# Pooling layer in channel order: one 512-wide product for both halves of the activation, and window sums as shifted additions

## The chip, the cores and the metric

The kernel runs on one core of a Trainium2 chip. The metric is the device time of one execution in microseconds; the time before is the median of three runs.

## The reference, cut to what matters

A token sequence (256 tokens, 2048 channels) passes a retention layer, a pooling layer and a second, longer block. The change is in the pooling layer:

```python
h = rms_norm(x, g_norm)                       # a factor for each token, one for each channel
u, z = jnp.split(h @ w_in, [POOL_WIDTH], axis=-1)
# four groups of 1024 channels, windows w = 2, 4, 8, 16
for gi, w in enumerate(POOL_WINDOWS):
    lo = jnp.maximum(t + 1 - w, 0)
    cnt = jnp.minimum(t + 1, w)
    pooled_gi = (cs[t + 1] - cs[lo]) / cnt    # mean of the last w tokens
mix = jnp.einsum('bsgc,gcd->bsgd', pooled - u, w_grp) + b_grp
out = (mix.reshape(B, S, POOL_WIDTH) * scale * silu(z)) @ w_out
```

## The kernel before

All weights come as one stream of 900 chunks of 256 x 512 numbers (512 KB). A chunk goes through five hands, each engine working its own program in order, and rings of four slots (`raw`, `whi`, `wlo`) couple them: SyncE starts the transfer into `raw`, ScalarE casts `raw` to `whi` (line 626), VectorE subtracts to get the rest `wlo` (line 1078), TensorE multiplies. ScalarE and VectorE prepare chunk j + 4 in iteration j, the cast waiting until TensorE has finished chunk j (`multiplied`), since that frees the slot. A product of full precision takes three matmuls: high x high, high x low, low x high. The activation too is held in two halves (`aH`, `aL`).

In `chunk_a` (lines 1930 to 1932) the activation is the stationary operand and the 512 columns of the chunk stream past it: 12 matmuls of 512 columns, and the result has a token on each partition. In `chunk_b` (lines 1955 to 1958, used in the second block) the weights are stationary and the 256 tokens stream: 24 matmuls of 256 columns, and the result has a channel on each partition. Both make the same products.

The pooling layer takes four groups of 40 chunks (`group`, `first` for group 0), then the product with the output weights (128 chunks of `chunk_a` on `oH`, `oL`). In a group, chunks 0 to 15 give u (two halves of 512 channels, `b` = 0 and 1), chunks 16 to 31 give z, chunks 32 to 39 multiply the pooled input by the group's weights. Before the change the pooling itself is a matrix product: after chunk 19, 32 matmuls (lines 2056 to 2059) take u, split into `pUH` and `pUL`, times a 256 x 256 band matrix `pMH`, and turn it into channel order. ScalarE makes `pUH` (line 660, scaled with each token's `rstd`), `pMH` (742) and then `mH` (747); VectorE makes `pUL` (1301) and `mL` (1308). At the end of each half of the group's product, in iterations 35 and 39, VectorE waits for the chunk, adds the bias in two instructions that read the result (`mz`, line 1320, semaphore `mz_add`), and gates with silu(z) (`pZ`, line 1328). In the next group's first 16 iterations it turns the result into `mz_turned` (line 1092) and splits it (`oL`, line 1114).

The order on every engine is what the code spells out; nothing is planned at run time.

Of the kernel before, what the change touches and what calls it, by code (L numbers as in the profile page):

```python
# [101 lines left out]
C_END = C_WIN + GROUPS * NT  # L102
# [7 lines left out]
def build(nc, dram):  # L110
    with ExitStack() as outer:
# [19 lines left out]
        aH = sb(outer, "aH", [P, 16, SEQ], F32R)  # L131
        aL = sb(outer, "aL", [P, 16, SEQ], F32R)
# [17 lines left out]
        with ExitStack() as s:  # L150
# [20 lines left out]
            with ExitStack() as r:  # L171
                with ExitStack() as b:
                    mz = sb(b, "mz", [P, NT, NB])
                    pB = sb(b, "pB", [P, GDIM])
                pUH = sb(r, "pUH", [P, NT, GDIM], F32R)
                pUL = sb(r, "pUL", [P, NT, GDIM], F32R)
# [5 lines left out]
                pM = sb(r, "pM", [P, 3 * P])  # L182
                pMH = sb(r, "pMH", [P, 3 * P], F32R)
# [7 lines left out]
        with ExitStack() as s:  # L191
# [89 lines left out]

        cum_rows = nc.dram_tensor("cum_rows", [NT, DN_HEADS, P], F32).ap()
# [27 lines left out]
        pu_sb, pu_lo, pz_sb, mix_ps, mix_hi, mix_lo, pm_in, pb_in, mz_add, mz_sb, pb_used = (  # L310
            sem(n) for n in "pu_sb pu_lo pz_sb mix_ps mix_hi mix_lo pm_in pb_in mz_add mz_sb pb_used".split())
# [189 lines left out]
        def _(pool):  # L501
# [79 lines left out]
            pool.wait_ge(const_set, 3)  # L581
# [37 lines left out]
        def _(act):  # L619
# [107 lines left out]
            def group(i, first):  # L727
                q = i * (P_PER // RING) + P_AT // RING
                for j in range(P_PER):
                    split_hi(q, j + RING)  # L730
                    if first and j == 1:
                        t_split_hi(T_N2 + 3, aH, 12, lambda c: C_PN + 12 + c)
                    if not first and j in (8, 16):
                        group_tail(i - 1, j // 8 - 1)
                    if j in (7, 15):
                        done(act, q, j)
                        b = j // 8
                        act.wait_ge(row_rstd, M_N2 + 1)
                        by_token(pUH[:, :, b * NB:(b + 1) * NB], 2 * b, ACT.Copy, M_N2, pu_sb)
                    if j == 16:  # L740
                        act.wait_ge(pm_in, i * 16 + 16)
                        nc.scalar.copy(pMH[:], pM[:]).then_inc(pu_sb, 1)
                    if j == 19:
                        act.wait_ge(t_lo, (T_P + 2 * i) * QT)
                        for b in range(4):
                            act.wait_ge(mix_ps, i * 4 + (b + 1))
                            nc.scalar.copy(mH[:, 2 * b:2 * b + 2].rearrange("p a n -> p (a n)"),
                                           PS[:, 4 + b]).then_inc(mix_hi, 1)
                    if j in (23, 31):
                        done(act, q, j)  # L750
                        b = j // 8 - 2
                        by_token(pZ[:, :, b * NB:(b + 1) * NB], 2 * b, ACT.Silu, M_N2, pz_sb)
# [173 lines left out]
            def first_tap(i):  # L926
# [6 lines left out]
                act.wait_ge(const_set, 4)  # L933
# [139 lines left out]
        def _(dve):  # L1073
# [212 lines left out]

            def group(i, first):
                q = i * (P_PER // RING) + P_AT // RING
                for j in range(P_PER):
                    split_lo(q, j + RING)  # L1290
                    if first and j == 1:
                        t_split_lo(T_N2 + 3, aH, aL, 12, lambda c: C_PN + 12 + c)
                    if not first:
                        after_group(i - 1, j, 2)
                    if j in (7, 15):

                        b = j // 8
                        dve.wait_ge(pu_sb, i * 3 + (b + 1))
                        for t in range(NT):
                            cut = pUH[:, t, b * NB:(b + 1) * NB].bitcast(F32)  # L1300
                            ins = nc.vector.scalar_tensor_tensor(out=pUL[:, t, b * NB:(b + 1) * NB], in0=PS[:, 2 * b + t],
                                                                 scalar=rstd[:, M_N2, t:t + 1], in1=cut, op0=ALU.mult,
                                                                 op1=ALU.subtract)
                        ins.then_inc(pu_lo, 1)
                    if j == 19:
                        for b in range(4):
                            dve.wait_ge(mix_hi, i * 4 + (b + 1))
                            nc.vector.tensor_tensor(mL[:, 2 * b:2 * b + 2].rearrange("p a n -> p (a n)"), PS[:, 4 + b],
                                                    mH[:, 2 * b:2 * b + 2].rearrange("p a n -> p (a n)").bitcast(F32),
# [604 lines left out]
        def _(pe):  # L1914
# [46 lines left out]

            def transpose_tiles(src, bank=6):
# [74 lines left out]
            def group(i, first):  # L2037
                q = i * (P_PER // RING) + P_AT // RING
                for j in range(4 * K16):
                    b = j // K16  # L2040
                    if j == 16 or j == 24:
                        pe.wait_ge(pu_lo, i * 2 + (b - 1))
                    if first and j == 6:
                        pe.wait_ge(t_lo, (T_N2 + 4) * QT)
                    chunk_a(q, j, (j % K16) * KPC, aH, aL, 2 * (b % 2), j % K16 == K16 - 1)
                    if first and j == 1:
                        pe.wait_ge(h_out, 2 + 4)
                        pe.wait_ge(t_lo, (T_N2 + 3) * QT)
                        transpose_tiles(quarter(H, 3))
                    if j == 19:  # L2050

                        pe.wait_ge(pu_lo, i * 2 + 2)
                        pe.wait_ge(pu_sb, i * 3 + 3)
                        for c in range(8):
                            out, ch = half(4, c), slice(c * P, (c + 1) * P)
# [432 lines left out]
```

## Time and profile before

| | |
|---|---|
| median of 3 runs | 2625.68 us (2625.46 to 2626.24) |
| span of the profiled execution | 2624.1 us |
| TensorE busy | 2608.1 us, 99% of the span |
| VectorE busy | 1960.0 us, 75% |
| ScalarE busy | 1321.0 us, 50% |
| DMA | 499.69 MB, 190 GB/s on average |

The profiled execution's own time is not given apart from the runs; the three runs stand 1.4 to 2.1 us above its span, which is what lies around first and last instruction. "Busy" of TensorE counts overlapped matmuls once; the duration of one matmul in the profile is its latency, so its pace has to be read from the starts of successive ones.

### The profile page before, as it was taken

What the parts mean: (1) busy time and instruction counts of PE and PEld (TensorE: products, weight loads), DVE (VectorE), ACT (ScalarE), POOL (GpSimd) and SP (SyncE); (2) the same over time, 40 slices, a digit from 0 to 9 for tenths busy, and PEclk for the clock granted to TensorE, in tenths of its full rate; (3) what the DMA queues carried; (4) which work ended last, traced back from release to release, by engine and by line L of the source; (5) the groups of instructions that cost most, each with busy time, mean ns of one, the idle gap of its engine ahead of it and who ended that gap; (6) DMA issues with size and microseconds to landing.
All of it is one profiled execution on the core that took longest, in us unless ns stands there. A gap on an engine that the chain in (4) does not pass through costs nothing.

```text
span 2624.1 us, 36684 instructions
## 1 busy us (share of the span) xinstructions
PE 2608.1 (99%) x13284; PEld 2218.9 (85%) x13284; DVE 1960.0 (75%) x2764; ACT 1321.0 (50%) x1683; POOL 168.0 (6%) x329
## 2 busy tenths in 40 slices
PE   9999999999999999999999999999999999999998
PEld 7888888888888888888889999998888888788887
DVE  5888877776755766757457786977798999989565
ACT  5444444444444544444456454454666666564453
POOL 0000000000000000000000341413000000000000
PEclk9999999999999999999999999999999999999999
DMA  8555555555655555556655555655555655655754
GB/s 309 179 187 177 179 185 185 184 191 190 198 193 192 195 196 192 196 185 217 196 189 176 173 165 159 194 159 175 176 197 191 197 192 187 200 188 194 247 175 159
DMA packets 151674, 499.69 MB, mean 190 GB/s; under 512 B 28736, under 2 KB 29472, under 8 KB 151008
## 3 DMA queue, kind: packets, MB, share of 16 engines
q1 hardware_dynamic: 148736, 486.18, 56.0%
q0 software_dynamic: 2784, 11.40, 1.4%
q8 instruction: 104, 1.70, 0.3%
q14 instruction: 50, 0.41, 0.0%
HBM read 493.30 MB, written 4.21 MB: 190 GB/s over the span
## 4 chain that ended last, share of the span: by engine, by line
PE 97%; DVE 2%; ACT 1%; issue 0%; DMA 0%; POOL 0%; SPq 0%; DVEq 0%; ACTq 0%
PE PS L1930 27%; PE PS L1932 27%; PE PS L1931 27%; PE PS L1955 4%; PE PS L1957 4%; PE PS L1958 4%; PE PS L2096 2%; DVE yl L1624 1%; DVE wlo L1078 0%; PE PS L2103 0%; PE PS L1966 0%; PE PS L2112 0%; DVE yl L1615 0%; PE PS L2010 0%; PE PS L2020 0%
## 5 line engine op out<-in xcount | busy, mean ns | idle before, releaser
L1078 DVE TENSOR_TENSOR wlo<-raw,whi 128x1024 fp32r<-128x1024 f32 x899 | 1096.9, 1225 | 595.8 <-ACT whi L626 591.1
L626 ACT CAST whi<-raw 128x1024 fp32r<-128x1024 f32 x899 | 939.6, 1049 | 1180.7 <-PE PS L1932 1009.4
L1930 PE MATMUL PS<-whi,aH 128*128 128x512 f32 x2160 | 844.1, 391 | 3.2 <-DVE wlo L1137 1.9
L1931 PE MATMUL PS<-wlo,aH 128*128 128x512 f32 x2160 | 840.6, 389 | 0.0
L1932 PE MATMUL PS<-whi,aL 128*128 128x512 f32 x2160 | 840.6, 389 | 0.0
L1930 PEld LDWEIGHTS PS<-whi,aH 128*128 128x128 f32 x2160 | 405.6, 188 | 88.1 <-issue 2.3
L1932 PEld LDWEIGHTS PS<-whi,aL 128*128 128x128 f32 x2160 | 405.5, 188 | 84.6
L1931 PEld LDWEIGHTS PS<-wlo,aH 128*128 128x128 f32 x2160 | 405.6, 188 | 82.9
L1955 PE MATMUL PS<-aH,whi 128*128 128x256 f32 x768 | 220.8, 288 | 1.5 <-DVE aL L1114 1.5
L1957 PE MATMUL PS<-aL,whi 128*128 128x256 f32 x768 | 217.1, 283 | 0.0
L1958 PE MATMUL PS<-aH,wlo 128*128 128x256 f32 x768 | 217.1, 283 | 0.0
L1932 PE MATMUL PS<-whi,oL 128*128 128x512 f32 x512 | 199.2, 389 | 0.0
L1930 PE MATMUL PS<-whi,oH 128*128 128x512 f32 x512 | 199.2, 389 | 0.0
L1931 PE MATMUL PS<-wlo,oH 128*128 128x512 f32 x512 | 199.2, 389 | 0.0
L1955 PEld LDWEIGHTS PS<-aH,whi 128*128 128x128 f32 x768 | 147.0, 191 | 2.5 <-issue 1.7
L1957 PEld LDWEIGHTS PS<-aL,whi 128*128 128x128 f32 x768 | 147.2, 192 | 0.1
L1958 PEld LDWEIGHTS PS<-aH,wlo 128*128 128x128 f32 x768 | 147.0, 191 | 0.0
L1624 DVE SCALAR_TENSOR_TENSOR yl<-up,wl,yl 128x256 f32<-128x256 f32 x272 | 113.3, 478 | 0.2
L1931 PEld LDWEIGHTS PS<-wlo,oH 128*128 128x128 f32 x512 | 96.1, 188 | 20.1
L1932 PEld LDWEIGHTS PS<-whi,oL 128*128 128x128 f32 x512 | 96.1, 188 | 20.1
L1930 PEld LDWEIGHTS PS<-whi,oH 128*128 128x128 f32 x512 | 96.1, 188 | 19.6
L1930 PE MATMUL PS<-whi,oaH 128*128 128x512 f32 x256 | 99.9, 390 | 0.0
(357 smaller groups left out, 2570.6 us busy)
## 6 DMA issues: line engine op xcount, KB each, us to landing
raw<-in_stream SPq DMA_DIRECT2D x900, 512.0 KB, 3.3
xT<-in_xT SPq DMA_DIRECT2D x4, 512.0 KB, 7.6
H<-in_x SPq DMA_DIRECT2D x4, 512.0 KB, 10.0
pB<-in_pool_b POOLq DMA_DIRECT2D x4, 512.0 KB, 4.5
iT<-diag_in SPq DMA_DIRECT2D x16, 128.0 KB, 3.7
bg<-in_b_gate POOLq DMA_DIRECT2D x8, 256.0 KB, 3.8
out<-eb SPq DMA_DIRECT2D x8, 256.0 KB, 2.2
dmask<-in_dmask SPq DMA_DIRECT2D x4, 384.0 KB, 5.8
```

The source lines that it names most:

```text
L626: nc.scalar.copy(whi[:, s], raw[:, s]).then_inc(hi_done, 1 + blank)
L1078: nc.vector.tensor_tensor(wlo[:, s], raw[:, s], whi[:, s].bitcast(F32), ALU.subtract).then_inc(lo_done, 1 + blank)
L1624: nc.vector.scalar_tensor_tensor(out=to, in0=up[:, c, k:k + SEQ], scalar=w, in1=yl[:, c], op0=ALU.mult, op1=ALU.add).then_inc(long_tap[c], 1)
L1930: mm(out, hi[:, kt + k, tok], whi[:, s, k], start=kt + k == 0, stop=False)
L1931: mm(out, hi[:, kt + k, tok], wlo[:, s, k], start=False, stop=False)
L1932: ins = mm(out, lo[:, kt + k, tok], whi[:, s, k], start=False, stop=last and k == KPC - 1)
L1955: mm(half(bank, c), whi[:, s, k, w], aH[:, kt + k], start=kt + k == 0 and c % 2 == 0, stop=False, skip_group_check=True)
L1957: mm(half(bank, c), whi[:, s, k, w], aL[:, kt + k], start=False, stop=False, skip_group_check=True)
L1958: ins = mm(half(bank, c), wlo[:, s, k, w], aH[:, kt + k], start=False, stop=end, skip_group_check=True)
L2096: ins = mm(PS[rows, bank + n, h * P + at:h * P + at + width], lhsT(t, h), rhs(t, h), start=h == 0, stop=True, skip_group_check=True)
```

## The change

- `aH` and `aL` become two interleaved parts of one tile `aHL`, so that both halves of the activation are 512 contiguous columns.
- u is computed by a new function `chunk_w`: weights stationary, a matmul of 512 columns for `whi` against both halves, one of 256 columns for `wlo` against the high half. The two halves of a bank are added on VectorE (`pU`), and then multiplied by a row of the tokens' `rstd` (`rrow`, fetched through DRAM).
- The band product is gone. VectorE forms window sums by 1, 2, 3 or 4 shifted additions between padded tiles (`window_sum`), subtracts size times u, and treats the first tokens apart.
- The eight PSUM banks are dealt out anew: u in banks 4 to 7 (b = 0) and 0 to 3 (b = 1), z in banks 4 to 7. TensorE gets new waits for that, `mz_add` among them: in front of chunk 8 of groups 1 to 3, and in front of the output product.

```diff
+ADD_AT = (9, 17)
+SUM_AT = ((11, 13, 15, 18, 19, 20), (21, 23, 24, 25, 26, 27))
+SPLIT_AT = (22, 29)
...
                     if j in (7, 15):
                         done(act, q, j)
                         b = j // 8
-                        act.wait_ge(row_rstd, M_N2 + 1)
-                        by_token(pUH[:, :, b * NB:(b + 1) * NB], 2 * b, ACT.Copy, M_N2, pu_sb)
-                    if j == 16:
-                        act.wait_ge(pm_in, i * 16 + 16)
-                        nc.scalar.copy(pMH[:], pM[:]).then_inc(pu_sb, 1)
-                    if j == 19:
+                        act.wait_ge(const_set, 3)
+                        if not first:
+                            act.wait_ge(mix_lo, i * 2 + (b - 1))
+                        nc.scalar.copy(pU[:, b, :, PAD:], wide(b)[:, :, SEQ:]).then_inc(pu_lo, 1)
+                    if j + 1 in SPLIT_AT:
+                        b = SPLIT_AT.index(j + 1)
                         act.wait_ge(t_lo, (T_P + 2 * i) * QT)
-                        for b in range(4):
-                            act.wait_ge(mix_ps, i * 4 + (b + 1))
-                            nc.scalar.copy(mH[:, 2 * b:2 * b + 2].rearrange("p a n -> p (a n)"),
-                                           PS[:, 4 + b]).then_inc(mix_hi, 1)
+                        act.wait_ge(pool_step, steps_before(i, b + 1))
+                        nc.scalar.copy(mH[:, b * QT:(b + 1) * QT], pU[:, b, :, PAD:]).then_inc(mix_hi, 1)
...
+            def window_sum(i, b, n):
+
+                at, early = steps_before(i, b) + n, POOL_WINDOWS[i] - 1
+                u = pU[:, b, :, PAD:]
+                if n == 0:
+                    if i == 0 and b == 0:
+                        dve.wait_ge(rrow_in, 32)
+                    dve.wait_ge(pu_sb, i * 2 + (b + 1))
+                    nc.vector.tensor_tensor(u, u, rrow[:, None, :].to_broadcast([P, QT, SEQ]), ALU.mult).then_inc(pool_step, 1)
+                    return
+                dve.wait_ge(pool_step, at)
+                shift = 1 << (n - 1)
+                v = pU[:, b] if n == 1 else pS[:, n % 2]
+                if n <= i + 1:
...
+                    nc.vector.tensor_tensor(pS[:, (n + 1) % 2, :, PAD:], v[:, :, PAD:], v[:, :, PAD - shift:PAD - shift + SEQ],
+                                            ALU.add).then_inc(pool_step, 1)
+                else:
...
+                    nc.vector.tensor_tensor(own_size, u[:, :, 0:early], sizes, ALU.mult).then_inc(pool_step, 1)
+                    nc.vector.scalar_tensor_tensor(out=u[:, :, early:], in0=u[:, :, early:], scalar=float(-POOL_WINDOWS[i]),
+                                                   in1=v[:, :, PAD + early:], op0=ALU.mult, op1=ALU.add).then_inc(pool_step, 1)
+                    dve.wait_ge(pool_step, at + 1)
+                    nc.vector.tensor_tensor(u[:, :, 0:early], own_size, v[:, :, PAD:PAD + early], ALU.add).then_inc(pool_step, 1)
...
+            def chunk_w(q, j, kt, b, last):
...
+                for k in range(KPC):
+                    for c in range(QT):
+                        w, out = slice(c * P, (c + 1) * P), wide(b)[:, c]
+                        mm(out, whi[:, s, k, w], aHL[:, kt + k].rearrange("p a n -> p (a n)"), start=kt + k == 0, stop=False,
+                           skip_group_check=True)
+                        ins = mm(out[:, 0:SEQ], wlo[:, s, k, w], aH[:, kt + k], start=False, stop=last and k == KPC - 1,
+                                 skip_group_check=True)
+                ins.then_inc(multiplied, 1)
...
             for i in range(1, P_N):
                 group(i, False)
+            pe.wait_ge(mz_add, P_N * 2)
             for b in range(4):
                 q = (PO_AT + b * K32) // RING
                 pe.wait_ge(h_out, 4 + b + 1)
```

TensorE, before: the pooling product behind chunk 19 of a group (`aH`, `aL` belong to the chunk, `pUH`, `pUL` and `pMH` to the product).

```order
L1930 MATMUL PS<-whi,aH 128x512
L1931 MATMUL PS<-wlo,aH 128x512
L1932 MATMUL PS<-whi,aL 128x512
L2056 MATMUL PS<-pMH,pUH 128x256 [waits pu_sb,pu_lo]
L2057 MATMUL PS<-pMH,pUL 128x256
L2058 MATMUL PS<-pMH,pUH 128x128
L2059 MATMUL PS<-pMH,pUL 128x128
L2056 MATMUL PS<-pMH,pUH 128x256
```

TensorE, now: the first rows of a chunk of u in `chunk_w`.

```order
L2018 MATMUL PS<-aHL,whi 128x512 [waits lo_done]
L2020 MATMUL PS<-aHL,wlo 128x256
L2018 MATMUL PS<-aHL,whi 128x512
L2020 MATMUL PS<-aHL,wlo 128x256
L2018 MATMUL PS<-aHL,whi 128x512
```

The 32 matmuls of the product have no successor on TensorE; a chunk of u has 16 matmuls (8 wide, 8 narrow) where it had 12 wide ones.

TensorE, before: the last matmuls of group 3 and the first of the output product.

```order
L1930 MATMUL PS<-whi,mH 128x512
L1931 MATMUL PS<-wlo,mH 128x512
L1932 MATMUL PS<-whi,mL 128x512
L1930 MATMUL PS<-whi,oH 128x512 [waits lo_done,h_out]
L1931 MATMUL PS<-wlo,oH 128x512
```

TensorE, now, at the same place.

```order
L1978 MATMUL PS<-whi,mH 128x512
L1979 MATMUL PS<-wlo,mH 128x512
L1980 MATMUL PS<-whi,mL 128x512
L1978 MATMUL PS<-whi,oH 128x512 [waits lo_done,h_out,mz_add]
L1979 MATMUL PS<-wlo,oH 128x512
```

The order is the same, but the first matmul of the output product now also waits for `mz_add`.

VectorE, before: group 3, iterations 16 to 39 (`wlo` is the split of a chunk).

```order
L1114 SCALAR_TENSOR_TENSOR oL<-mz_turned,cols,oH 128x256 [waits t_hi] x4
L1078 TENSOR_TENSOR wlo<-raw,whi 128x1024 [waits hi_done] x3
L1308 TENSOR_TENSOR mL<-PS,mH 128x512 [waits mix_hi] x4
L1078 TENSOR_TENSOR wlo<-raw,whi 128x1024 [waits hi_done] x16
L1320 SCALAR_TENSOR_TENSOR mz<-PS,cols,pB 128x512 [waits mz_sb,pb_in,multiplied]
```

VectorE, now: group 3, iterations 17 to 22.

```order
L1351 TENSOR_TENSOR pU<-PS,pU 128x4x256 [waits pu_lo]
L1103 TENSOR_TENSOR wlo<-raw,whi 128x1024 [waits hi_done]
L1328 TENSOR_TENSOR pS<-pS 128x4x256 [waits pool_step]
L1103 TENSOR_TENSOR wlo<-raw,whi 128x1024 [waits hi_done]
L1328 TENSOR_TENSOR pS<-pS 128x4x256 [waits pool_step]
L1103 TENSOR_TENSOR wlo<-raw,whi 128x1024 [waits hi_done]
L1333 TENSOR_TENSOR pS<-pU,cols 128x4x15 [waits pool_step]
L1334 SCALAR_TENSOR_TENSOR pU<-pU,pS 128x4x241
L1337 TENSOR_TENSOR pU<-pS 128x4x15 [waits pool_step]
L1103 TENSOR_TENSOR wlo<-raw,whi 128x1024 [waits hi_done]
L1320 TENSOR_TENSOR pU<-pU,rrow 128x4x256 [waits pu_sb]
L1103 TENSOR_TENSOR wlo<-raw,whi 128x1024 [waits hi_done]
```

Where VectorE did split after split, a full-size instruction now stands behind each split.

## Rows read from the trace of the kernel before

**Rows 1.** The page: span, busy time and granted clock in 40 slices.
```profile
span 2624.1 us, 36684 instructions
...
PE 2608.1 (99%) x13284; PEld 2218.9 (85%) x13284; DVE 1960.0 (75%) x2764; ACT 1321.0 (50%) x1683; POOL 168.0 (6%) x329
...
PEclk9999999999999999999999999999999999999999
```

**Rows 2.** Waits of PE in the whole span: us in total, times, longest.
```profile
PE PS L1930 <- DVE wlo L1137: 1.9, 1, 1.9
...
PE PS L1930 <- DVE wlo L1078: 1.4, 1, 1.4
```

**Rows 3.** Timeline of PE around group 0's pooling product: start, duration (us).
```profile
788.75 0.28 PE L2056 MATMUL PS<-pMH,pUH 128*128 128x256 f32 x1
...
789.15 0.33 PE L2056 MATMUL PS<-pMH,pUH 128*128 128x256 f32 x1
789.32 0.28 PE L2057 MATMUL PS<-pMH,pUL 128*128 128x256 f32 x1
...
792.40 0.45 PE L1930 MATMUL PS<-whi,aH 128*128 128x512 f32 x1
792.68 0.40 PE L1931 MATMUL PS<-wlo,aH 128*128 128x512 f32 x1
```

**Rows 4.** Tile pUH: min/median/max ns, first and last start (us).
```profile
L2056 PE MATMUL PS<-pMH,pUH x32: 277/332/333, 788.7 to 1129.5; 128*128 128x256 f32 x32
```

**Rows 5.** Timeline where the last group ends and the output product begins.
```profile
1184.45 0.39 PE L1930 MATMUL PS<-whi,oH 128*128 128x512 f32 x1
...
1184.71 1.05 ACT L626 CAST whi<-raw 128x1024 fp32r<-128x1024 f32 x1 [1.67 <-PE PS L1932]
...
1185.79 1.23 DVE L1078 TENSOR_TENSOR wlo<-raw,whi 128x1024 fp32r<-128x1024 f32 x1 [1.50 <-ACT whi L626]
...
1186.93 1.40 DVE L1320 SCALAR_TENSOR_TENSOR mz<-PS,cols,pB 128x512 f32<-128x512 f32 x2
...
1187.17 0.39 PE L1930 MATMUL PS<-whi,oH 128*128 128x512 f32 x1
```

**Rows 6.** Timeline of PE in chunk_b: a chunk, first row to next.
```profile
1374.03 0.28 PE L1955 MATMUL PS<-aH,whi 128*128 128x256 f32 x1
...
1376.91 1.03 PE L1966 MATMUL PS<-con,XS 128*128 128x128 f32 x8
```

**Rows 7.** Timeline: a stall of PE that a wlo ends.
```profile
2261.78 1.21 DVE L1078 TENSOR_TENSOR wlo<-raw,whi 128x1024 fp32r<-128x1024 f32 x1
...
2263.05 0.50 PE L1930 MATMUL PS<-whi,aH 128*128 128x512 f32 x1 [1.37 <-DVE wlo L1078]
...
2263.38 0.40 PE L1931 MATMUL PS<-wlo,aH 128*128 128x512 f32 x1
...
2263.62 0.39 PE L1932 MATMUL PS<-whi,aL 128*128 128x512 f32 x1
```

**Rows 8.** Groups between 720 and 1260 us: count, busy us, mean ns, idle before.
```profile
L1078 DVE TENSOR_TENSOR wlo<-raw,whi 128x1024 fp32r<-128x1024 f32 x193 | 235.9, 1225 | 184.4 <-ACT whi L626 183.7
L626 ACT CAST whi<-raw 128x1024 fp32r<-128x1024 f32 x193 | 202.0, 1049 | 276.5 <-PE PS L1932 275.5 <-DMA raw<-in_stream 0.9
...
L1092 DVE STREAM_TRANSPOSE mz_turned<-pZ 32x256 f32<-32x256 f32 x128 | 55.8, 436 | 2.5
...
L1114 DVE SCALAR_TENSOR_TENSOR oL<-mz_turned,cols,oH 128x256 fp32r<-128x256 f32 x32 | 13.3, 478 | 0.0
...
L1320 DVE SCALAR_TENSOR_TENSOR mz<-PS,cols,pB 128x512 f32<-128x512 f32 x16 | 11.2, 743 | 0.0
...
L1347 DVE TENSOR_TENSOR H<-PS,H 128x1024 f32<-128x1024 f32 x1 | 1.2, 1218 | 0.0
```

**Rows 9.** Windows at the start: us, then busy us (x instructions) by engine, PEclk, DMA.
```profile
3.00:4.00 1.00, 1.00 (x7) 1.00 (x7) 0.00 (x0) 0.00 (x0) 0.00 (x0) 1.00 0.97 181
...
5.00:6.00 1.00, 1.00 (x12) 1.00 (x11) 0.00 (x0) 0.09 (x1) 0.00 (x0) 1.00 1.00 360
```

More of the change, by code:

```diff
@@ L366, in half, with wide, steps_before @@
             return PS[:, bank + c // 2, (c % 2) * SEQ:(c % 2 + 1) * SEQ]
+        def wide(b):
+            return PS[:, 4 - 4 * b:8 - 4 * b]
+        def steps_before(i, b):
+            return sum(2 * (g + 5) for g in range(i)) + b * (i + 5)
         def heads(bank):
@@ L932, in first_tap @@
                 act.wait_ge(up_sb, i + 1)
-                act.wait_ge(const_set, 4)
+                act.wait_ge(const_set, 5 + P_N)
                 act.wait_ge(wl_set, i + 1)
@@ L1291, in group @@
                     if first and j == 1:
-                        t_split_lo(T_N2 + 3, aH, aL, 12, lambda c: C_PN + 12 + c)
+                        t_split_lo(T_N2 + 3, aH, aL, 12, lambda c: C_PN + 12 + c, 0)
                     if not first:
                         after_group(i - 1, j, 2)
[L1295 to L1309, printed above, removed]
+                    for b in range(2):
+                        if j == ADD_AT[b]:
+                            dve.wait_ge(pu_lo, i * 2 + (b + 1))
+                            u = pU[:, b, :, PAD:]
+                            nc.vector.tensor_tensor(u, wide(b)[:, :, 0:SEQ], u, ALU.add).then_inc(pu_sb, 1)
+                        if j in SUM_AT[b][:i + 3]:
+                            window_sum(i, b, SUM_AT[b].index(j))
+                        if j == SPLIT_AT[b]:
+                            dve.wait_ge(mix_hi, i * 2 + (b + 1))
+                            nc.vector.tensor_tensor(mL[:, b * QT:(b + 1) * QT], pU[:, b, :, PAD:],
+                                                    mH[:, b * QT:(b + 1) * QT].bitcast(F32),
                                                     ALU.subtract).then_inc(mix_lo, 1)
@@ L2040, in group @@
                     b = j // K16
-                    if j == 16 or j == 24:
-                        pe.wait_ge(pu_lo, i * 2 + (b - 1))
+                    if j == 0:
+                        if not first:
+                            pe.wait_ge(pz_sb, i * 2)
+                    if j == K16 and not first:
+                        pe.wait_ge(mz_add, i * 2)
+                    if b >= 2 and j % K16 == 0:
+                        pe.wait_ge(pu_sb, i * 2 + (b - 1))
                     if first and j == 6:
                         pe.wait_ge(t_lo, (T_N2 + 4) * QT)
-                    chunk_a(q, j, (j % K16) * KPC, aH, aL, 2 * (b % 2), j % K16 == K16 - 1)
+                    if b < 2:
+                        chunk_w(q, j, (j % K16) * KPC, b, j % K16 == K16 - 1)
+                    else:
+                        chunk_a(q, j, (j % K16) * KPC, aH, aL, 2 * b, j % K16 == K16 - 1)
                     if first and j == 1:
@@ L2048, in group @@
                         pe.wait_ge(t_lo, (T_N2 + 3) * QT)
[L2049 to L2055, printed above, removed]
-                            mm(out, pUH[:, 0, ch], pMH[:, 0:SEQ], start=c % 2 == 0, stop=False, skip_group_check=True)
-                            mm(out, pUL[:, 0, ch], pMH[:, 0:SEQ], start=False, stop=False, skip_group_check=True)
-                            mm(out[:, P:], pUH[:, 1, ch], pMH[:, SEQ:], start=False, stop=False, skip_group_check=True)
-                            ins = mm(out[:, P:], pUL[:, 1, ch], pMH[:, SEQ:], start=False, stop=True,
-                                     skip_group_check=True)
-                            if c % 2:
-                                ins.then_inc(mix_ps, 1)
-                pe.wait_ge(mix_lo, i * 4 + 4)
+                        transpose_tiles(quarter(H, 3), 0)
                 for w in range(2):
-                    pe.wait_ge(pz_sb, i * 2 + (w + 1))
                     for k in range(4):
+                        if not w and k % 2 == 0:
+                            pe.wait_ge(mix_lo, i * 2 + (k // 2 + 1))
                         chunk_a(q, 4 * K16 + 4 * w + k, k * KPC, mH, mL, 2 * w, k == 3)
```

63 lines of the change are left out of this document (40 added, 23 removed).

## Prediction

> **What bounds the kernel now.** First the page: TensorE is busy 2608.1 of 2624.1 us, at full clock in all 40 slices [rows 1]. Then TensorE's waits: the longest is 1.9 us, at the start, and the one behind it 1.4 us, near 2263 us; none lies in the pooling stage [rows 2]. So nobody but TensorE sets the end: a microsecond that it is spared or made to idle there is a microsecond of the result, and work on the other engines costs nothing until it makes TensorE wait. Its pace comes from starts, since durations overlap: a chunk of `chunk_a`, 12 matmuls of 512 columns, takes from 1184.45 to 1187.17, 2.72 us [rows 5]. In the stage VectorE is idle 184 us ahead of its splits and ScalarE 277 us ahead of its casts, nearly all of it until TensorE frees a slot [rows 8]. That is the cover for what the change adds on them.
>
> **The pooling product goes.** Its first matmul starts at 788.75, chunk 20 at 792.40: 3.65 us. The first matmul of chunk 20 is followed after 0.28 us where 0.23 is usual, 0.05 more [rows 3]. 32 of L2056 [rows 4], eight to a group, make four such products. 4 x 3.70 = 14.8 us saved, all on the path.
>
> **A chunk of u gets four more matmuls for the same columns.** 8 x 512 + 8 x 256 = 6144 = 12 x 512. What the split costs is read from `chunk_b`, which has the same 6144 columns in 24 matmuls: 1374.03 to 1376.91, 2.88 us [rows 6]. That is 0.16 us over `chunk_a` for 12 matmuls more, 13.3 ns each. Four more make 0.053 us, on 4 x 16 = 64 chunks 3.4 us. No row shows a wide and a narrow matmul in turn with weights on both. Bounds: nothing (columns alone count), and the longest spacing of a 256-column one, 0.17 us (789.15 to 789.32), which follows a 128-column one [rows 3]; against 0.12 in `chunk_b` that is 0.05 x 8 x 64 = 26 us. I take 3.4, since here every narrow matmul stands behind a wide one, longer than the 0.12 at which `chunk_b` gets its weights in.
> The Trainium skill, "TensorE: Matmul & The Clock Gate", section "Back-to-back issue gap", gives a start-to-start gap of N / 2.4 + 2.5 ns at full clock. By that an extra matmul costs 2.5 ns, the 64 chunks 0.6 us, and the sum below would end 2.8 us lower. The rows disagree with it here (13 ns a matmul), and I go by them.
>
> **The wait in front of the output product.** TensorE's program now has `wait_ge(mz_add, P_N * 2)` ahead of the first matmul on `oH`, that is, it waits for the last `mz` of group 3. VectorE makes that in iteration 39, behind the split of chunk 43, which waits for the cast, which waits until TensorE is through with chunk 39. The rows give the whole chain, as nothing in it changes: TensorE could go on at 1184.45; cast from 1184.71, split from 1185.79, the two `mz` from 1186.93 for 1.40, to 1188.33 [rows 5]. Before, TensorE multiplied through this (chunks 40 and 41), since banks 0 and 1 had been read in iteration 35. Now it idles 3.88 us. Leaving a stall costs more: in the one at 2263 the split ends at 2262.99, TensorE starts at 2263.05, and the next start comes after 0.33 instead of 0.23, the one after it 0.24 [rows 7]: 0.06 + 0.11. Together 4.05 us. Nothing gives it back, as TensorE has no slack behind it; what is queued behind the waiting matmul is the entire output product. ScalarE and VectorE only gain time by it.
>
> **The other new waits of TensorE** cost nothing. `mz_add` at chunk 8 of groups 1 to 3 asks for the same event, 3.9 us after the end of chunk 39, with 8 x 2.72 = 21.8 us to spare it. `pz_sb` at chunk 0: silu of iteration 31. `pu_sb` at chunks 16 and 24: the additions of iterations 9 and 17, six chunks earlier. `mix_lo` at chunks 32 and 34: splits in iterations 22 and 29; the later starts, undelayed, 1.34 + 1.23 us after chunk 29 ends [rows 5] and takes 1.22, so 3.8 of the 10.9 us (four chunks) to chunk 34's start.
>
> **VectorE.** It loses eight `pUL` pieces' worth and the `mL` ones read from PSUM; it gains full-size (128 x 1024) instructions: per half of a group the addition, the scaling, i + 1 shifted sums, the subtraction, and the split of the mix, 2 x (5 + i), so 10, 12, 14, 16 = 52, and two tiny ones per half. Durations: 1.23 between SBUF tiles (the split itself), 1.22 with one operand in PSUM (`H`), and for the scalar form 0.743 at 512 columns and 0.478 at 256, which carried on to 1024 makes 1.27 [rows 8]. The tiny ones I take as 0.12 with their waits.
> Worst is group 3. A split is ready 2.57 us after its slot's chunk ends (1184.45 to 1187.02) and needed three chunks after, 8.16: cover 5.6 us. The delay d grows by an iteration's work less 2.72. Iteration 8: 1.23 + 0.88 of turning + 4 x 0.478 = 4.0, d = 1.3. Iteration 9, split, turning, addition: 3.33, d = 1.9; 10: 2.1, d = 1.3; 11, 13, 15 add 0.6 each, 12 and 14 give it back: 1.9 before 16; 16: 3.1, d = 2.3; from 17 to 27 each 2.45, d falls by 0.27 an iteration but for 20 and 27, which are near 2.8. So the highest delay is some 2.3 of 5.6 us, and it is gone before iteration 35. ScalarE waits in iterations 21 and 28 for the end of a chain of sums, about 1 us behind its usual time, and has 277 us of idle time around it. With d at 2.3 a slot's refill starts 2.3 us later than its usual place, against four chunks of time to land. I cost all this at nothing.
> Where the cover ends: from iteration 8 to 29 of group 3 there are 22 x 2.72 + 5.6 = 65.4 us for 22 x 1.23 + 8 x 0.88 + 8 x 0.478 = 37.9 us of old work and 16 new instructions: 1.7 us each. Group 2 has 14 for the same room, 1.96 each.
>
> **ScalarE and GpSimd.** ScalarE trades 16 `pUH`, 4 `pMH` and 16 `mH` for 16 instructions of 128 x 1024 of the cast's size, 1.05 [rows 8]: less work. `rrow` needs two small transfers after group 0 begins; the first scaling is in iteration 11, 30 us later.
>
> **Sum.** -14.8 + 3.4 + 4.05 = -7.35 us. Against the profiled span 2624.1 that is 2616.75; the runs stand 1.4 to 2.1 us above the span, and from their median, 2625.68, I get 2618.3, 0.28% less. A measurement of this kernel can tell about 0.2%, 5.3 us, from no change, so the border of faster is 2620.4.
>
> **Rivals.**
> 1. *The wait is not felt* (7 in 100): the event is there in time. Against it: split and `mz` follow each other without a gap in rows 5. Then -11.4, 2614.3.
> 2. *The stall drops TensorE's clock* (12 in 100). At the start the warming matmuls come 7 in a microsecond, two microseconds later 12 in one [rows 9], so an engine that comes from idleness works at the lower of its levels (1.2 GHz instead of 2.4) for a while. The longest waits of TensorE inside the kernel are 1.4 and 1.9 us and the clock stays at full [rows 1, 2]; this one is 3.9. If a stretch as long as that first one, about 3 us, runs at half speed, 1.5 us is lost: 2619.8, still faster. The same page of the Trainium skill, section "Why this matters for your kernels", warns that a gap between bursts puts the clock back; no row here shows it for a gap inside the kernel.
> 3. *VectorE becomes the bound* (8 in 100): the place is iterations 8 to 29 of groups 2 and 3, where the full-size sums stand behind every split. It needs instructions of over 1.7 us. At 2.45, twice the row, groups 3, 2 and 1 overrun by 16 x 2.45 - 27.5 = 11.7, 6.8 and 1.9 us, 20 in all: 2638, slower. The gain is eaten at 2.08 us each: 5.8 + 1.6 = 7.4. For it: two of the three operands are in one padded tile, some reads are shifted, and VectorE goes on for 12 iterations with 0.27 us of slack each. Against it: the 128 x 1024 rows shown, with both operands in SBUF or one in PSUM, stand at 1.22 and 1.23 [rows 8].
> 4. *Narrow matmuls take 0.17 us* (5 in 100): the 26 us above, so 2641, slower.
> 5. *The change does not do what it says*, no gain from the product (2 in 100): not with its 32 matmuls gone from the order.
>
> **How the numbers follow.** The forecast itself has 66 in 100, 2618.3, its own range 2616.5 to 2620.2 (13.3 ns a matmul read to 0.01 us, the stall to 0.3 us). The range goes down to rival 1 with a part of the four extra matmuls' price off (2613.5), and up to rival 2 with a stall or two behind VectorE of 1 us each (2622.0); it leaves out rivals 3 to 5 and a rest, some 2 in 10. Faster takes the forecast and rivals 1 and 2, less what lies above 2620.4: 0.79. Slower takes rivals 3 and 4 without VectorE's mild cases: 0.11. The rest, 0.10, is same.
>
> **What would show it.** Right: no L2056 to L2059 rows; chunks of u at 2.77 us; one wait of TensorE, 3.9 to 4.1 us, in front of the output product, ended by VectorE's `mz`; no other wait of TensorE between 740 and 1180 us; full-size rows of VectorE at 1.2 to 1.3 us; the end of the groups' stage 14.8 - 3.4 = 11.4 us earlier than before. Wrong: TensorE rows with idle time ended by `wlo` inside a group, spacings of 256-column matmuls over 0.13 us, or spacings of 512-column ones near 0.43 behind the stall.

## The result, and the profile after

| | before | after |
|---|---|---|
| median, both on one chip, 5 runs each | 2625.73 us (2625.46 to 2627.24) | 2645.68 us (2642.90 to 2646.42) |
| span of the profiled execution | 2624.1 us | 2644.5 us |
| ratio after / before | | 1.0071 [1.0059, 1.0083] |

The change makes the kernel slower by 0.7%. The forecast was 2618.3, with a range up to 2622.0; the result is outside of it, on the other side of no change.

The page of the changed kernel, the parts that answer to [rows 1]:

```profile
span 2644.5 us, 36952 instructions
PE 2622.4 (99%) x13412; PEld 2221.8 (84%) x13412; DVE 2000.2 (76%) x2800; ACT 1317.2 (50%) x1663; POOL 163.1 (6%) x332
PEclk9999999999999999999999999999999999999999
```

TensorE is as busy as before, only for longer. Its waits, against [rows 2]:

```profile
engine line waited for: us in total, times, longest us
PE PS L1978 <- DVE mz L1368: 3.8, 1, 3.8
PE PS L2170 <- DVE iT L1477: 2.4, 3, 0.9
PE PS L1978 <- DVE wlo L1162: 2.2, 1, 2.2
PE PS L2003 <- DVE aHL L1139: 1.4, 1, 1.4
```

The first is the forecast stall. The second, three waits of 0.7 to 0.9 us for `iT`, is in the second block and was not forecast. Together they are a few microseconds, where 27.75 are to be explained (2644.5 against the 2616.75 of the sum). The timeline of TensorE around the stall:

```profile
start us, us, engine line op out<-in xcount [idle before <-releaser]
1184.17 0.39 PE L1980 MATMUL PS<-whi,mL 128*128 128x512 f32 x1
1188.33 0.50 PE L1978 MATMUL PS<-whi,oH 128*128 128x512 f32 x1 [3.77 <-DVE mz L1368]
1188.67 0.39 PE L1979 MATMUL PS<-wlo,oH 128*128 128x512 f32 x1
1188.90 0.40 PE L1980 MATMUL PS<-whi,oL 128*128 128x512 f32 x1
...
1192.04 0.63 PE L1980 MATMUL PS<-whi,oL 128*128 128x512 f32 x1
1192.47 0.63 PE L1978 MATMUL PS<-whi,oH 128*128 128x512 f32 x1
1192.89 0.52 PE L1979 MATMUL PS<-wlo,oH 128*128 128x512 f32 x1
```

and VectorE's at the same place, against the end of [rows 5]:

```profile
1185.73 1.22 DVE L1103 TENSOR_TENSOR wlo<-raw,whi 128x1024 fp32r<-128x1024 f32 x1 [1.57 <-ACT whi L651]
1186.88 1.40 DVE L1368 SCALAR_TENSOR_TENSOR mz<-PS,cols,pB 128x512 f32<-128x512 f32 x2
```

TensorE starts again 4.16 us after the matmul before it, where 0.23 is usual. A little over a microsecond after TensorE goes on, its matmuls come 0.43 apart. The windows view says why (the number behind the count is the granted clock):

```profile
1184.00:1194.00 10.00, 6.23 (x21) 0.83 0.39 125
1189.80:1193.10 3.30, 3.30 (x9) 0.50 0.06 21
```

The rest has no wait and no clock in it. It is in the pace of 512-column matmuls that the change doesn't touch. The grouped view of the output product's stretch 1205 to 1345, one kind of its three matmuls, before and then after:

```profile
L1930 PE MATMUL PS<-whi,oH 128*128 128x512 f32 x207 | 80.5, 389 | 0.0
```

```profile
L1978 PE MATMUL PS<-whi,oH 128*128 128x512 f32 x201 | 79.6, 396 | 0.0
```

In the same 140 us, 620 matmuls were done before (three kinds) and 602 now. A matmul lasts 7 ns longer (396 for 389), and from start to start the mean goes from 226.7 to 233.3 ns. Comparing when the stages begin, by first starts of TensorE in both traces, shows where it adds up:

| TensorE starts | before | after | later by |
|---|---|---|---|
| first product on `oH` | 559.37 | 560.28 | 0.91 |
| first chunk of u | 733.45 | 739.48 | 6.03 |
| could begin the output product | 1184.45 | 1184.40 | -0.05 |
| first `chunk_b` of the second block | 1367.35 | 1377.99 | 10.64 |
| output product of the second block, on `oaH` | 1899.11 | 1912.32 | 13.21 |
| first product on `ubH` | 2343.30 | 2358.64 | 15.34 |
| first product on `pTh` | 2518.30 | 2538.72 | 20.42 |

The pooling groups, where the change works, gain 6.1 us. Five microseconds are lost before them, in the products on `oH` from 559 on, and the rest behind them.

Two readings on the forecast's other worries. A chunk of u, wide and narrow matmuls in turn:

```profile
1084.15 0.40 PE L2018 MATMUL PS<-aHL,whi 128*128 128x512 f32 x1
1084.38 0.28 PE L2020 MATMUL PS<-aHL,wlo 128*128 128x256 f32 x1
1084.50 0.40 PE L2018 MATMUL PS<-aHL,whi 128*128 128x512 f32 x1
1084.74 0.28 PE L2020 MATMUL PS<-aHL,wlo 128*128 128x256 f32 x1
1084.86 0.40 PE L2018 MATMUL PS<-aHL,whi 128*128 128x512 f32 x1
```

A wide matmul is followed after 0.23 or 0.24 us, a narrow one after 0.12; two pairs take 0.71 us, and the eight pairs of a chunk 2.83.

VectorE's groups between 735 and 1230, against [rows 8]:

```profile
L1103 DVE TENSOR_TENSOR wlo<-raw,whi 128x1024 fp32r<-128x1024 f32 x176 | 215.2, 1224 | 125.6 <-ACT whi L651 125.0
L1328 DVE TENSOR_TENSOR pS<-pS 128x1024 f32<-128x1024 f32 x12 | 14.6, 1220 | 0.1
L1320 DVE TENSOR_TENSOR pU<-pU,rrow 128x1024 f32<-128x1024 f32 x8 | 9.8, 1222 | 0.0
L1351 DVE TENSOR_TENSOR pU<-PS,pU 128x1024 f32<-128x1024 f32 x8 | 9.8, 1220 | 0.0
L1334 DVE SCALAR_TENSOR_TENSOR pU<-pU,pS 128x964 f32<-128x964 f32 x2 | 2.3, 1158 | 0.0
```

The full-size rows stand at 1.22 us and VectorE still has 125.6 us of idle time ahead of its splits.

### The profile page after: what moved, and what is told of

The parts are those of the page before. It is cut to its first block, busy times and chain, and to the rows that moved or that the text cites. A ratio compares the mean times of both kernels' runs of the same rounds, so it can differ in the third digit from the quotient of the medians.

```text
span 2644.5 us, 36952 instructions
## 1 busy us (share of the span) xinstructions
PE 2622.4 (99%) x13412; PEld 2221.8 (84%) x13412; DVE 2000.2 (76%) x2800; ACT 1317.2 (50%) x1663; POOL 163.1 (6%) x332
## 3 DMA queue, kind: packets, MB, share of 16 engines
q8 instruction: 105, 1.72, 0.3%
## 4 chain that ended last, share of the span: by engine, by line
PE 90%; POOL 3%; DVE 3%; DMA 2%; issue 1%; SPq 1%; ACT 1%; DVEq 0%; ACTq 0%; POOLq 0%
PE PS L1978 24%; PE PS L1980 24%; PE PS L1979 24%; PE PS L2018 5%; PE PS L2020 2%; PE PS L2003 2%; PE PS L2005 2%; PE PS L2006 2%; POOL xi L594 2%; PE PS L2154 2%; POOL xt L590 2%; DVE wlo L1103 1%; DVE yl L1672 1%; DMA iT<-diag_in 0%; PE PS L2028 0%
## 5 line engine op out<-in xcount | busy, mean ns | idle before, releaser
L1978 PE MATMUL PS<-whi,aHL 128*128 128x512 f32 x1904 | 745.3, 391 | 3.5 <-DVE wlo L1162 2.2
L1980 PE MATMUL PS<-whi,aHL 128*128 128x512 f32 x1904 | 742.2, 390 | 0.0
L1979 PE MATMUL PS<-wlo,aHL 128*128 128x512 f32 x1904 | 742.0, 390 | 0.0
L1978 PEld LDWEIGHTS PS<-whi,aHL 128*128 128x128 f32 x1904 | 357.7, 188 | 78.2 <-issue 2.3
L1980 PEld LDWEIGHTS PS<-whi,aHL 128*128 128x128 f32 x1904 | 357.6, 188 | 74.5
L1979 PEld LDWEIGHTS PS<-wlo,aHL 128*128 128x128 f32 x1904 | 357.8, 188 | 73.1
L2003 PE MATMUL PS<-aHL,whi 128*128 128x256 f32 x768 | 221.2, 288 | 1.4 <-DVE aHL L1139 1.4
L2005 PE MATMUL PS<-aHL,whi 128*128 128x256 f32 x768 | 217.6, 283 | 0.0
L2006 PE MATMUL PS<-aHL,wlo 128*128 128x256 f32 x768 | 217.5, 283 | 0.0
L2018 PE MATMUL PS<-aHL,whi 128*128 128x512 f32 x512 | 180.5, 398 | 0.0
L2003 PEld LDWEIGHTS PS<-aHL,whi 128*128 128x128 f32 x768 | 147.3, 192 | 2.5 <-issue 1.7
L2005 PEld LDWEIGHTS PS<-aHL,whi 128*128 128x128 f32 x768 | 147.5, 192 | 0.1
L2006 PEld LDWEIGHTS PS<-aHL,wlo 128*128 128x128 f32 x768 | 147.4, 192 | 0.0
L2020 PE MATMUL PS<-aHL,wlo 128*128 128x256 f32 x512 | 144.0, 281 | 0.0
```

Of the source, the lines that this page charges most:

```text
L1978: mm(out, hi[:, kt + k, tok], whi[:, s, k], start=kt + k == 0, stop=False)
L1979: mm(out, hi[:, kt + k, tok], wlo[:, s, k], start=False, stop=False)
L1980: ins = mm(out, lo[:, kt + k, tok], whi[:, s, k], start=False, stop=last and k == KPC - 1)
L2003: mm(half(bank, c), whi[:, s, k, w], aH[:, kt + k], start=kt + k == 0 and c % 2 == 0, stop=False, skip_group_check=True)
L2005: mm(half(bank, c), whi[:, s, k, w], aL[:, kt + k], start=False, stop=False, skip_group_check=True)
L2006: ins = mm(half(bank, c), wlo[:, s, k, w], aH[:, kt + k], start=False, stop=end, skip_group_check=True)
```

## The experiments

**The theory.** Which matmuls have slowed can be told by the tile that is stationary: those on `aHL` run at 227 ns as before, those on `oH`, `mH`, `oaH`, `ubH` and `pTh` at 233. The tiles lie one behind the other in SBUF, the memory from which the engines read, and `cols`, the tile of constants, grows in the change by 16 columns, 64 bytes, for the window sizes (`C_NSZ` in the diff). `raw`, `whi`, `wlo`, `H` and the activation lie ahead of `cols` and stay; everything behind moves by 64 bytes. In the built program before, `whi`, `wlo`, `aH`, `oH`, `mH`, `oaH` and `ubH` all start 128 bytes past a multiple of 256 in a partition; now those behind `cols` start at 192. The theory: a 512-column matmul is slower by 6 ns or so where its two tiles, the stationary one and the one that streams past it, don't start alike, that is, the same number of bytes past a multiple of 256. The rivals: the slowdown comes with the change's new work (SBUF or PSUM traffic of VectorE and ScalarE), or with `chunk_w` and the half clock.

**e1, the kernel before with 16 unused columns, and e2, with 32.** Nothing else is changed; the tiles behind `cols` move by 64 and by 128 bytes.

```
-C_END = C_WIN + GROUPS * NT
+C_END = C_WIN + GROUPS * NT + 16
```

> The kernel before, with 16 unused columns (64 bytes a partition) at the end of cols, and nothing else. Layout theory: every tile laid out behind cols starts 64 bytes later, as in the changed kernel; matmuls whose stationary tile lies there (oH, oL, mH, mL, oaH, oaL, ubH, ubL, about 3,070 of them) go from 226.7 to 233.3 ns, 20 us, and TensorE waits some 2 us longer for iT; together 2646 to 2649 us, as slow as the changed kernel although nothing of the change is in it. Rival (the slower pace comes from the interleaved aHL, the new VectorE work or the new code): 2625.7 us, paces of 227 ns everywhere but on pEh.

> The control: 32 unused columns, so the same tiles start 128 bytes later. Layout theory in the form 'off a multiple of 128 bytes is slow': 2625.7 us within 1 us, oH at 227 ns. Rival form (any shift or a larger cols costs): 2646 us or more.

e1: 2646.49 us (2646.13 to 2646.82), ratio 1.0075 [1.0058, 1.0092]. The whole loss appears without any of the change's work, and with the same pace: 602 matmuls in 1205 to 1345, 233.3 ns on `oH`, 226.9 on `aH`. The rivals fall as causes of the pace. e2: 2643.22 us, ratio 1.0063 [1.0046, 1.0080], 604 matmuls, 232.4 ns. So 128 bytes do not restore it.

A small product tests the theory further: `vH` and `vL` on `sTH` and `sTL`, 72 matmuls in groups of nine. All four tiles lie behind `cols` and start alike in every kernel here. In e2 they keep their pace but for the ends of a group, where the neighbour is a matmul on `aH` or `aL` (227.8 ns on average, 225 to 228 inside). In e1 they don't: 231.0 on average, with single spacings from 224 to 236. Six spacings in e1, then six in e5 (the kernel before with every tile 128 bytes later, see below):

```profile
135.07 0.40 PE L2021 MATMUL PS<-vH,sTL 128*128 128x512 f32 x1
...
136.46 0.40 PE L2021 MATMUL PS<-vH,sTL 128*128 128x512 f32 x1
```

```profile
134.53 0.39 PE L2022 MATMUL PS<-vH,sTL 128*128 128x512 f32 x1
...
135.90 0.39 PE L2022 MATMUL PS<-vH,sTL 128*128 128x512 f32 x1
```

So after a move by 64 bytes matmuls lose pace though their tiles still start alike, and "not alike" does not cover that case.

**e3, the changed kernel with `cols` 16 columns wider still, and e4, the same without the stall.** e4 asks at first only for the `mz` that the first quarter's banks need, and for the last one ahead of the second quarter.

```
-            pe.wait_ge(mz_add, P_N * 2)
+            pe.wait_ge(mz_add, P_N * 2 - 1)
             for b in range(4):
...
+                if b == 1:
+                    pe.wait_ge(mz_add, P_N * 2)
```

> The changed kernel with 16 more unused columns, 128 bytes in all, so that the tiles behind cols start on a multiple of 128 again. Layout theory: 20.5 us for the stationary tiles and some 2 us of the iT waits come back: 2645.7 - 22.5 = 2623 us, below the kernel before by about 0.1%. Rival (the change itself is slow): 2645.7 us stays.

> As the one before it, and the wait ahead of the output product asks for mz_add 7 (banks 0 and 1 read), with 8 asked for only ahead of b = 1, whose banks 2 and 3 those are. If the stall is 4.1 us and the half clock behind it 1.7 us: 5.8 us less than the aligned one, 2617 us, clock at full throughout. Rival (the stall was hidden in what follows): no difference.

e3: 2639.07 us (2637.21 to 2640.83), ratio 1.0048 [1.0032, 1.0065]; 605 matmuls. It is what e2 showed: 128 bytes off is nearly as slow as 64 off. The form of the theory in which 128 bytes are enough had missed, in both runs. e4: 2632.30 us (2631.14 to 2633.40, 10 runs), ratio 1.0020 [1.0010, 1.0030]: the stall is gone. But the profiled execution has a stretch of 3.41 us at half clock from 1367.3. It begins at the end of the second of two gaps of 0.89 and 1.72 us from start to start, which stand in the profile of before as well and are followed there by full clock. In e4's windows (granted clock 0.83 over ten microseconds, as behind the stall above):

```profile
1365.00:1375.00 10.00, 8.55 (x60) 0.83 0.80 242
```

**Place or distance: e5 and e6.** For the 128 bytes two forms of the theory were left: the place of a tile in 256 bytes counts, or the distance between the stationary and the streaming tile. e5 is the kernel before with an unused tile of 128 bytes ahead of all others: each place changes, no distance does. In e6 `raw`, `whi` and `wlo` and the tiles from `oH` on start at multiples of 256, while `aH` and `aL` stay 128 past one; `ssq` and `ms` are allocated ahead of `H` for it.

```
+        shift = sb(outer, "shift", [P, 32])
         raw = sb(outer, "raw", [P, RING, KPC, NB])
...
+        ssq = sb(outer, "ssq", [P, 6, NT])
+        ms = sb(outer, "ms", [P, 6, NT])
         H = sb(outer, "H", [P, NT, DM])
```

(e5 has the first added line alone; e6 has all three, and leaves out the old lines of `ssq` and `ms`.)

> The kernel before, with an unused tile of 128 bytes a partition ahead of every tile, so that the stationary (aH, oH and the rest) and the streaming ones (whi, wlo) all start 128 bytes later: at a multiple of 256 where they stood 128 behind one. Theory 'distance': what counts is that stationary and streaming tile start alike modulo 256; then nothing changes, 2626 us, 227 ns. Theory 'place': the start of the stationary tile itself must be 128 behind a multiple of 256; then aH and aL go to 232.4 ns as well, as oH did in the run with 32 columns, and some 10,000 matmuls cost 5.7 ns each, 57 us: about 2684 us.

> The kernel before, with 128 bytes ahead of raw, whi and wlo (now at a multiple of 256), and two small tiles (ssq, ms: 128 bytes) moved from behind aL to in front of H, so that H, aH and aL stand 128 behind a multiple of 256 as before, and oH, mH, oaH, ubH at a multiple. 'Distance': aH and aL are now unlike whi and go to 232.4 ns (some 6,500 matmuls, 37 us), oH is like whi and stays at 227: 2663 us. 'Place': the other way round, aH at 227, oH at 232.4, 2643 us as with 32 columns.

e5: 2626.25 us (2625.76 to 2627.59), ratio 0.9998 [0.9988, 1.0007], the matmuls on `aH`, `oH`, `mH`, `oaH` and `ubH` at 226 to 227 ns. Place falls for a move by 128 bytes; one of 64 for all tiles was not tried. e6: 2660.06 us (2658.82 to 2660.93), ratio 1.0125 [1.0110, 1.0141]; the slow and the quick tiles have changed sides. One kind of matmul on `aH` between 300 and 440, which now lasts 395 ns:

```profile
L1931 PE MATMUL PS<-whi,aH 128*128 128x512 f32 x192 | 75.9, 395 | 0.0
```

From start to start the matmuls on `aH` and `aL` take 232.4 ns, on `oH`, `mH`, `oaH` and `ubH` 226 to 227. For 128 bytes that is the distance, in both directions. For 64 bytes the runs do not tell distance from place, and the product on `sTH` in e1 speaks against distance alone.

**e7, the changed kernel with the sizes in a tile of their own, and e8, the same with e4's wait.** `cols` has its old width, and `nsz` lies in the pooling layer's part of SBUF, behind all tiles that TensorE reads there.

```
-C_NSZ = C_WIN + GROUPS * NT
-C_END = C_NSZ + POOL_WINDOWS[-1]
+C_END = C_WIN + GROUPS * NT
...
+                nsz = sb(r, "nsz", [P, POOL_WINDOWS[-1]])
...
+            pool.dma_start(nsz[:], dram["sizes"]).then_inc(nsz_in, 16)
...
+                        dve.wait_ge(nsz_in, 16)
...
-                    sizes = cols[:, C_NSZ:C_NSZ + early][:, None, :].to_broadcast([P, QT, early])
+                    sizes = nsz[:, 0:early][:, None, :].to_broadcast([P, QT, early])
```

> The changed kernel with its 16 window sizes in a tile of their own in the pooling layer's memory, loaded by a transfer of its own, so that cols has its old width and every tile of the other layers its old place. Both forms of the layout theory: oH, mH, oaH, ubH back to 227 ns, 20 us less than 2645.7, and the wide matmuls of u at or below 232; 2622 to 2624 us with the stall ahead of the output product and one stretch of half clock behind it. Rival (the new code has a cost of its own beside the layout): over 2630 us.

> The same, and the wait ahead of the output product asks for mz_add 7, the 8 only ahead of b = 1. The stall of 4.1 us and the half clock behind it (1.7 us) go: 2616.5 us, 0.35% below the kernel before. Rival: the clock falls elsewhere instead, 2618.5 us; or the stall was covered, 2622 us.

e7: 2624.50 us (2622.68 to 2627.10, 10 runs), ratio 0.9991 [0.9982, 1.0001]. The pace is back, and with it 21 us:

```profile
L1981 PE MATMUL PS<-whi,oH 128*128 128x512 f32 x207 | 80.5, 389 | 0.0
```

TensorE's stall and the half clock behind it stay, as e7's windows show (the clock is the 0.50):

```profile
1181.60:1184.80 3.20, 3.20 (x9) 0.50 0.14 51
```

e8: 2617.96 us (2617.37 to 2618.15), ratio 0.9965 [0.9952, 0.9979], so faster than the kernel before by 0.35%. TensorE goes from `mL` to `oH` without a gap, and the clock stays full behind it. Between the medians of e7 and e8 lie 6.5 us, between the profiled spans 5.1:

```profile
1176.84 0.39 PE L1983 MATMUL PS<-whi,mL 128*128 128x512 f32 x1
1177.07 0.39 PE L1981 MATMUL PS<-whi,oH 128*128 128x512 f32 x1
```

**e9, e8 with a chunk of u in another order:** for each half of a chunk, first the four wide matmuls and then the four narrow ones.

```
                         mm(out, whi[:, s, k, w], aHL[:, kt + k].rearrange("p a n -> p (a n)"), start=kt + k == 0, stop=False,
                            skip_group_check=True)
+                    for c in range(QT):
+                        w, out = slice(c * P, (c + 1) * P), wide(b)[:, c]
                         ins = mm(
```

> The aligned kernel with the mended wait, and in chunk_w the four wide matmuls of a k first, then the four narrow ones, in place of wide and narrow in turn. There a wide one takes 236 ns and the narrow one behind it 117, 2.82 us a chunk where the forecast had 2.77. Theory 'alternation costs': 8 x 227 + 8 x 120 = 2.776 us a chunk, 64 chunks x 0.05 = 3 us less, 2615 us. Rival (the 512 columns of aHL cost by themselves, 236 ns in any order): 8 x 236 + 8 x 120, 2618 us or a little more.

2616.84 us (2616.37 to 2619.22), ratio 0.9965 [0.9951, 0.9979], not to be told from e8. The trace shows the small difference:

```profile
1077.93 1.09 PE L2021 MATMUL PS<-aHL,whi 128*128 128x512 f32 x4
1078.86 0.63 PE L2025 MATMUL PS<-aHL,wlo 128*128 128x256 f32 x4
1079.33 1.09 PE L2021 MATMUL PS<-aHL,whi 128*128 128x512 f32 x4
```

Half a chunk takes 1.40 us (1077.93 to 1079.33), a chunk 2.80, against 2.83 in e8. A wide matmul is followed after 232.1 ns instead of 236.4, a narrow one after 118.4 instead of 116.8. The theory had 227 and 2.776, the rival no gain, so neither came true. The span is 1.3 us shorter, 64 chunks of 0.03 being 1.9.

The traces of e3 and e4 show that the order is not all. There the chunks of u, with wide and narrow in turn as in e8, take 2.77 us in all four groups (231.7 and 115.0 ns), though `aHL`, `whi` and `wlo` lie where they lie in e8; only tiles that these matmuls don't read have moved. Four pairs in e3, 1.39 us:

```profile
1080.28 0.39 PE L2018 MATMUL PS<-aHL,whi 128*128 128x512 f32 x1
...
1081.67 0.39 PE L2018 MATMUL PS<-aHL,whi 128*128 128x512 f32 x1
```

In the changed kernel itself the first two chunks of group 0 take 2.82 and 2.83; then come eight short matmuls on `con` (745.14 to 745.90), and from the fourth chunk on each takes 2.77. So the places of its own tiles do not alone set the pace of a matmul. What else does was not tried.

**e10 and e11, how much VectorE could have taken:** e8 with 2, and with 4, unused additions of 128 x 512 ahead of each of the 20 shifted sums. Their results go to a tile that nobody reads.

```
+                    for _ in range(2):
+                        dve.wait_ge(warm, 1 + spares[0])
+                        nc.vector.tensor_tensor(spare[:], v[:, 0:2, PAD:], v[:, 2:4, PAD:], ALU.add).then_inc(warm, 1)
+                        spares[0] += 1
                     nc.vector.tensor_tensor(pS[:, (n + 1) % 2, :, PAD:], v[:, :, PAD:],
```

> The aligned kernel with the mended wait, and ahead of each shifted sum two unused additions of 128 x 512 (0.69 us and some 0.1 us of waiting each), to find where VectorE's cover ends. By the prediction's bound (27.5 us of room in iterations 8 to 29 of a group): group 3 has 16 x 1.22 + 8 x 1.6 = 32.3, 4.8 us too much, group 2 26.7, nothing: 2618 + 5 = 2623 us, with TensorE waiting for wlo in group 3 alone. Rival (VectorE's idle time is all usable): 2618 us, no waits.

> The same with four unused additions ahead of each sum. By the bound: group 3 45.1 - 27.5 = 17.6 us, group 2 36.3 - 27.5 = 8.8 us, group 1 27.4, nothing: 2618 + 26 = 2644 us, waits in groups 2 and 3. Rival: under 2625 us.

e10: 2620.21 us (2619.01 to 2621.44), ratio 0.9975 [0.9966, 0.9985], 2.3 us over e8. e11: 2640.66 us (2640.27 to 2641.04), ratio 1.0053 [1.0035, 1.0072], 22.7 us over e8 (2 runs only). Now TensorE waits for splits; from 850 to 1200 in e11:

```profile
engine line waited for: us in total, times, longest us
PE PS L1988 <- DVE wlo L1106: 15.7, 12, 2.1
```

and the busy time by group, the last window with group 3 and the start of the output product (behind the length of the window: TensorE's busy time, its weight loads', VectorE's, ScalarE's, GpSimd's, then the granted clock):

```profile
740.00:850.00 110.00, 110.00 (x545) 92.93 (x544) 71.39 (x72) 49.26 (x52) 3.15 (x7) 1.00 0.68 195
850.00:960.00 110.00, 109.42 (x538) 91.88 (x537) 92.98 (x118) 50.20 (x56) 0.68 (x2) 1.00 0.59 194
960.00:1070.00 110.00, 104.29 (x509) 86.59 (x509) 97.54 (x124) 48.79 (x54) 0.68 (x2) 1.00 0.56 182
1070.00:1200.00 130.00, 120.55 (x573) 99.02 (x572) 112.54 (x141) 52.79 (x59) 0.68 (x2) 0.99 0.53 176
```

The idle time is in groups 2 and 3 (5.7 and 9.5 us), and another 3.41 us at half clock begin at 1168.4, among the last of these waits. The unused addition takes 0.69 us.

## Why the prediction was wrong, by its steps

**The step that failed is one that the prediction does not have.** It cost the change part by part, and gave to every 512-column matmul that is not in the diff the pace of before. The line that widens `cols` stands in the diff and was costed at nothing, without a word. It moves the tiles of some 3,100 matmuls (1,536 on `oH` and `oL`, 768 on `oaH`, 384 on `mH`, 384 on `ubH` and a few on `pTh`) by 64 bytes against `whi` and `wlo`. (The two products on `oH` have 64 chunks each, 1184 to 1358 us in the second; the text on the kernel before gives 128.) At 233.3 for 226.7 ns each that is 3,100 x 6.6 = 20.5 us, the greater part of the 27.75 by which the span missed the sum's 2616.75. e1 shows the loss alone (2644.9 in the span, 20.8 over before's), e7 shows the change without it.

**The pooling product: right.** No row of it is left. Of the 11.4 us that the prediction saw saved by 1184, 6.1 are seen in the trace between the first chunk of u and the end of the groups: 384 matmuls on `mH` at 6.6 ns more take 2.5, and the chunks of u 2.5 more than forecast; that leaves 0.3 open.

**The chunk of u: right in kind, too small.** The narrow matmul is not the trouble (117 ns, inside the 0.12 of `chunk_b`), so rival 4 is out. The wide one is: in front of a narrow one it has 236.3 ns instead of 226.9 in groups 1 to 3, and 230.9 in group 0. A chunk takes 8 x 236.3 + 8 x 117.0 = 2.83 us where 2.77 was forecast; group 0 has 2.78 on average. The term is 16 x 0.057 + 48 x 0.103 = 5.9 us where 3.4 stood. The price itself, 13.3 ns for an extra matmul, is met in e3 and e4 with their 2.77, so it was not too low as such; the chunk has two paces, and what picks one stays open. e9 takes a part of it back.

**The stall: right.** 4.16 less the usual 0.23 is 3.93, and the next start comes 0.11 late (1188.33 to 1188.67), 4.04 together; 4.05 was forecast, ended by VectorE's `mz` as said. That it was needless shows in e8, where TensorE waits for one `mz` less and never stands still.

**Rival 2 came true** (12 in 100): 8 matmuls at 0.427 behind the stall cost 8 x 0.2 = 1.6 us where 1.5 was written. The half level at the start, on which that price was built, was read from 7 and 12 matmuls in a microsecond; the clock column of [rows 9] gives 1.00 in both. The stretch at 1189.8 shows it in the column too, 0.50. The Trainium skill, "TensorE: Matmul & The Clock Gate", section "Why this matters for your kernels", warns that idle gaps between bursts of matmuls put the clock back; the trace agrees at this stall of 3.77 us.

**VectorE: right, with a bound that is too tight.** No wait for `wlo` stands inside the stage, rival 3 did not happen. For group 3 the prediction had 27.5 us of room for 16 instructions. e11 adds 8 x 4 x 0.69 = 22.1 to 16 x 1.22 = 19.5, so TensorE should idle 14.1 us there, and idles 9.5; in group 2 it is 6.2 against 5.7. In e10 it should be 3.1 and is 1.0. So the room is larger by 0.5 to 5 us. The idle time appears where the prediction saw it, in the groups with the most sums.

**The sum again, with what the runs showed:** 2624.1 - 14.8 + 5.9 + 4.0 + 1.6 + 20.5 = 2641.3, and 2.3 for the waits for `iT` makes 2643.6 of 2644.5. Those waits stand in this profile of the changed kernel alone; before and e1 to e9 don't have them (e10 has one of 0.2 us, e11 one of 0.9). Nothing was tried on them, and their cause is open. For e7 the same sum without the 20.5 and the waits, and with all four groups at 2.83 (64 x 0.103 = 6.6), gives 2621.5; its span is 2621.7.

## What to carry to other kernels

Where TensorE sets the end, its pace is a part of the cost of every edit that resizes or moves a tile: before costing the parts of a change, list which tiles change their start, and afterwards compare the mean start-to-start time of matmuls that nobody touched. A few bytes of constants at the end of an early tile cost more here than the whole change saves; put such additions behind the tiles that matmuls read (padding `cols` to 256 bytes, which would keep every place modulo 256, was not tried). And a wait on a counter should ask for the event that the next instruction needs, not for the last one: one number in a wait was worth 5.1 us of span here (e7 to e8).

## What the runs showed of the hardware

- 512-column matmuls of one form ran at 226 to 227 ns from start to start where the stationary and the streaming tile start a multiple of 256 bytes apart in a partition, both of them at a multiple of 128; at 233.3 where one of them is 64 bytes off, and at 232.4 where it is 128 off. Each was seen in two kernels or more (before, e5 and e7; e1 and after; e2, e3 and e6). Tiles that start alike but 64 bytes past a multiple of 128 were seen only in the 72 matmuls on `sTH` and `sTL`: 231.0 on average in e1 and in after, 226.7 in before and e5. Already before, the 24 matmuls on `pEh` and `pEl`, which start 32 bytes past a multiple of 256 where `whi` is at 128, ran at 231 to 238 by kind. What in the chip makes it so was not shown; nor was any other distance tried. The Trainium skill, "SBUF — State Buffer", section "Operand start alignment", asks a tile's start only to be a multiple of the element's size and says that this is about legality, not speed.
- A wide matmul whose tiles start alike took 236 ns with a narrow one behind it in e7, e8, e10, e11 and three groups of after, but 231.7 in e3 and e4, with its tiles in the same places; and 232.1 on average when three of four are followed by another wide one (e9).
- Behind a stall of about 4 us the clock went to half for 3.41 us (after, e7), from 1.4 and 1.1 us after TensorE went on; in e3 for 6.83 us, from 1.7 us before it went on. At the two gaps of 0.89 and 1.72 us it stayed full in ten of the thirteen profiled executions (that of e8 among them) and fell for 3.41 us in those of e4, e5 and e6. That belongs to the execution and not to the kernel: of e5's ten runs three had a mean granted clock of 0.998, the profiled one among them, and spans of 2625.5 to 2626.2 us, the seven others 0.999 and 2624.3 to 2625.2; the kernel before had 0.998 in 8 of the 21 runs beside them. What decides there was not found.
